# Modulation products in full precision in four column groups of TensorE, with unsplit weights, in the setup and the first retrieval

## The chip, the cores and the metric

The kernel runs on one core of one Trainium2 chip. The metric is the device time of the whole program in microseconds (us). The kernel's time is the median over executions of it.

## The reference, cut to what matters

One inference step of a small trunk with two layers: 128 context tokens and 512 latent tokens, model width 1024. Both layers are modulated: a conditioning vector (`c` for the latent tokens, `c_ctx` for the context tokens) gives shift, scale and gate through a matrix of 1024 x 6144 for each layer.

```python
def _adaln(cvec, w, b):
    mod = jax.nn.silu(cvec) @ w + b
    return jnp.split(mod, 6, axis=-1)

for l in range(DEPTH):
    sh1p, sc1p, g1p, sh2p, sc2p, g2p = _adaln(c_ctx[None, :], ada_w[l], ada_b[l])
    sh1s, sc1s, g1s, sh2s, sc2s, g2s = _adaln(c, ada_w[l], ada_b[l])
    # a token mixer (gated linear recurrence) on the modulated, normed tokens,
    # then the expert mixer on the modulated, normed result:
    #   q = h @ w_q; scores against two sets of 128 sub-keys for each of 8 heads;
    #   top 16 of each, top 16 of the pairs; 16 experts of 16384 per head and token
```

The change touches only how `silu(cvec) @ w` is formed: two vectors against all 6144 columns, once for each layer.

## The kernel before, in words

**Stages.** The program runs stage after stage, with a barrier of all engines between them: `setup`, then for each of the two layers `mixer`, `mix_out`, `retrieve`, `route`, `experts`, and at the end `finish`. In each stage every engine has its own list of instructions and waits on semaphores. SP (the sync engine) only issues transfers, in the order of its list, and a wait in that list holds back every transfer behind it.

**Full float32 products by halves.** A weight tile `w` is split into `hi` (rounded to the format fp32r, on ScalarE) and `lo = w - hi` (on VectorE in `setup`, on GpSimd in `retrieve`), and TensorE multiplies the parts in fp32r. The vectors are split as well: `cs4` holds four columns for each slice of 128 rows, `hi` of both vectors and `lo` of both, so that the modulation's output has four rows (`pa`, `pm`), which a small product with the matrix `fold` adds up and turns into columns (`turn` at L377, `turn_row` at L1655).

**`setup` (L161 to L389).** It loads `ada_w` of layer 0 in 12 blocks of 512 columns (2 MB each) into a ring of four tiles `ada` (L211). From the fifth block on, SP waits until VectorE has made `ada_lo` of the block four before (L209). For each block ScalarE makes `ada_hi` in two halves (`split`, L339), VectorE `ada_lo` in two halves (L316), TensorE 8 + 8 products with a moving operand of 512 columns (L394), ScalarE copies the result row (`mod_row`, L355), TensorE turns it (L382), VectorE adds the bias (L308). Between the blocks ScalarE squares x (L344) and GpSimd adds the squares (L237). Ahead of it, VectorE makes `cs` and `cs4` (L294 to L300), which TensorE waits for.

**`retrieve` of layer 0 (L1451 to L1722).** A head has two steps (b = 0, 1), 16 steps in all; step s = 2h + b. In it TensorE projects all 640 tokens on 128 columns of `w_q`, in two halves of 24 products of 128x320 (P, L497; P of step 0 is at L487), and multiplies the result with the 128 sub-keys (scores S, L1633). VectorE takes the top 16 of the scores (L1683 to L1693), and once per head of the candidate pairs (L1707 to L1716). On the side, the modulation of layer 1 is made in 16 blocks of 384 columns (1.5 MB), one a step: product M (L1651), copy of the row (L1576), turn T (L1659), copy (L1582). In the second retrieval (layer 1, `later` false) this part doesn't exist. The lists are written out by hand:

- TensorE: P(s), S(s-1), M(s-1), P(s+1), S(s), M(s), and so on; T(s-2) stands in the middle of P(s), between its halves (L1623), so right behind M(s-2) come one half of P(s), then T(s-2).
- ScalarE, step s of its loop (L1594): row of M(s-2) (L1576), `ada_hi` of block s (L1570), copy of T(s-2), the copies of the projection of step s, `w_hi` of step s+2 (L1556).
- GpSimd: `ada_lo` (L1536) and `w_lo` (L1530), in turn.
- SP, step s (L1509 to L1520), three transfers: `w_raw` of step s (after `w_lo` of s-2), the keys `kraw`, `ada` of block s (after `ada_lo` of block s-2). Below, D(s) is the transfer of `ada` block s and W(s) that of `w_raw` of step s; W(s+1) stands right behind D(s).

```python
                    if later:
                        sp.wait_ge(ada_lo_done, h * 2 + (b + 1))
                        sp.dma_start(ada[b][:, :, :], ada_w[:, :, bass.ds(h * (2 * AW) + b * AW, AW)]) \
                            .then_inc(ada_in[b], 16)
```

Of the kernel before, what the change touches and what calls it, by code (L numbers as in the profile page):

```python
# [16 lines left out]
P = 128  # L17
# [79 lines left out]
def build_program(nc, a, out, upto=99):  # L97

    x_sp = nc.dram_tensor("xT_spill", [P, DC, T], F32, kind="Internal").ap()
    og_sp = nc.dram_tensor("og_spill", [DC, P, T], F32, kind="Internal").ap()  # L100
    gates_dram = nc.dram_tensor("gates", [KEYS, P, TD], F32, kind="Internal").ap()

    ctx = ExitStack()
    with ctx:
        c = {}
        for name, shape, dt in [
            ("ident", [P, P], F32), ("ones_d", [P, P], F32), ("ones_h", [P, P], F32),
            ("coarse_mask", [P, NT, P], BF16), ("fine_mask", [P, NF, FINE], BF16), ("room", [P, 624], F32),
            ("vec", [P, 3 * P], F32), ("mod", [P, DEPTH, 48, 2], F32), ("one", [P, 1], F32),
            ("scale_w", [P, DC, 2], F32), ("ident_r", [P, P], F32R),  # L110
            ("cs4", [P, DC, 4], F32R), ("fold", [P, 32], F32), ("lb", [P, 16], F32), ("oml", [P, 16], F32),
            ("x", [P, DC, T], F32), ("acc", [P, T], F32), ("inv", [P, PH * NT], F32),
        ]:
# [47 lines left out]
def setup(nc, a, c, x_sp, x_saved):  # L161
# [4 lines left out]
    with ExitStack() as s:  # L166
# [5 lines left out]
        ada_lo = [sb(f"ada_lo{i}", [P, DC, NB], F32R) for i in range(2)]  # L172
        ada_hi = [sb(f"ada_hi{i}", [P, DC, NB], F32R) for i in range(2)]
        cs = sb("cs", [P, 2, DC])
        cs4, fold = c["cs4"], c["fold"][:, 0:2]
# [17 lines left out]
        ada_hi_done, ada_lo_done = sem("ada_hi_done"), sem("ada_lo_done")  # L193
# [9 lines left out]
        HALF_K = (slice(0, DC // 2), slice(DC // 2, DC))  # L203

        @block.sync
        def _(sp):
            for n in range(NALL):
                if n >= 4:
                    sp.wait_ge(ada_lo_done, 2 * (n - 3))  # L209
# [6 lines left out]
        def _(pool):  # L216
# [7 lines left out]
            pool.memset(fold[:, :], 0.0)  # L224
            pool.drain()
            pool.affine_select(out=fold[:, :], in_=fold[:, :], compare_op=ALU.not_equal,
                               fill=1.0, base=0, pattern=[[-1, 2]], channel_multiplier=1)
            pool.drain()
            pool.affine_select(out=fold[:, :], in_=fold[:, :], compare_op=ALU.not_equal,
                               fill=1.0, base=-2, pattern=[[-1, 2]], channel_multiplier=1)  # L230
# [29 lines left out]
        def _(dve):  # L260
# [32 lines left out]
            for v, name in ((0, "c"), (1, "c_ctx")):  # L293
                nc.vector.tensor_mul(cs[:, v, :], sg[:, v, :], c["vec"][:, VEC[name]:VEC[name] + DC])  # L294
            dve.drain()
            for v in range(2):
                nc.vector.tensor_copy(cs4[:, :, v], cs[:, v, :])
            dve.drain()
            for v in range(2):
                nc.vector.tensor_sub(cs4[:, :, 2 + v], cs[:, v, :], cs4[:, :, v].bitcast(F32))  # L300
# [10 lines left out]
            for n in range(NALL):  # L311
                for i, ks in enumerate(HALF_K):
                    dve.wait_ge(ada_hi_done, 2 * n + i + 1)
                    if n >= 2 and i == 0:
                        dve.wait_ge(ada_mm, n - 1)
                    nc.vector.tensor_sub(ada_lo[n % 2][:, ks, :], ada[n % 4][:, ks, :],  # L316
                                         ada_hi[n % 2][:, ks, :].bitcast(F32)).then_inc(ada_lo_done, 1)
                if n >= 2:
                    add_bias(n - 2)
            add_bias(NALL - 2)  # L320
            add_bias(NALL - 1)
# [3 lines left out]
        def _(act):  # L325
# [8 lines left out]
            def split(n):  # L334
                act.wait_ge(ada_in[n % 4], n // 4 * 16 + 16)
                if n >= 2:
                    act.wait_ge(ada_mm, n - 1)
                for ks in HALF_K:
                    act.activation(ada_hi[n % 2][:, ks, :], ada[n % 4][:, ks, :], ACT.Copy).then_inc(ada_hi_done, 1)  # L339

# [5 lines left out]
            split(0)  # L346
            for n in range(NALL):
                if n + 1 < NALL:
                    split(n + 1)
# [5 lines left out]
                act.activation(mod_row[n % 2][0:4, :], pa[n % 2][0:4, :], ACT.Copy).then_inc(row_out, 1)  # L355

        @block.tensor
        def _(pe):
# [18 lines left out]
            def turn(n):  # L377
# [3 lines left out]
                for i in range(NB // P):  # L381
                    last = nc.tensor.matmul(pc[n % 2][:, i, :], mod_row[n % 2][0:4, i * P:(i + 1) * P], fold[0:4, 0:2],  # L382
# [3 lines left out]
            for n in range(NALL):  # L386
                if n >= 2:
                    pe.wait_ge(row_out, n - 1)
                for w, done in ((0, ada_hi_done), (1, ada_lo_done)):  # L389
                    part = (ada_hi, ada_lo)[w][n % 2]  # L390
                    for k in range(DC):
                        if k % 4 == 0:
                            pe.wait_ge(done, 2 * n + k // 4 + 1)
                        last = nc.tensor.matmul(pa[n % 2][0:4, :], cs4[:, k, :], part[:, k, :],  # L394
                                                start=(w == 0 and k == 0), stop=(w == 1 and k == DC - 1))
# [1055 lines left out]
def retrieve(nc, a, c, h_hi, h_lo, chosen, layer):  # L1451
# [10 lines left out]
    with ExitStack() as s:  # L1462
# [27 lines left out]
        if later:  # L1490
            ada_w = a["ada_w"][layer + 1].rearrange("(k p) n -> p k n", p=P)
            ada = [sb(f"ada{i}", [P, DC, AW]) for i in range(2)]
            ada_hi = [sb(f"ada_hi{i}", [P, DC, AW], F32R) for i in range(2)]
            ada_lo = [sb(f"ada_lo{i}", [P, DC, AW], F32R) for i in range(2)]
# [4 lines left out]
            ada_hi_done, ada_lo_done, ada_mm, row_out, row_turned, mod_done = (sem(n) for n in  # L1499
                ("ada_hi_done", "ada_lo_done", "ada_mm", "row_out", "row_turned", "mod_done"))  # L1500
# [7 lines left out]
        def _(sp):  # L1508
            with sp.Fori(0, PH) as h:  # L1509
                for b in range(2):  # L1510
# [6 lines left out]
                    if later:  # L1517
                        sp.wait_ge(ada_lo_done, h * 2 + (b + 1))
# [4 lines left out]
        def _(pool):  # L1523
            pool.sem_inc(w_lo_done, 2)
            if later:
                pool.sem_inc(ada_lo_done, 2)
# [6 lines left out]
            def ada_low(h, b):  # L1533
                if later:
                    pool.wait_ge(ada_hi_done, h * 2 + (b + 1))
                    pool.tensor_tensor(ada_lo[b][:, :, :], ada[b][:, :, :], ada_hi[b][:, :, :].bitcast(F32),  # L1536
                                       ALU.subtract).then_inc(ada_lo_done, 1)

            low(0, 0)
            low(0, 1)  # L1540
            with pool.Fori(0, PH - 1) as h:
                for b in range(2):
                    ada_low(h, b)
                    low(h + 1, b)
            ada_low(PH - 1, 0)
            ada_low(PH - 1, 1)

        @block.scalar
        def _(act):
# [17 lines left out]
            def ada_high(h, b):  # L1567
                if later:
                    act.wait_ge(ada_in[b], h * 16 + 16)
                    act.activation(ada_hi[b][:, :, :], ada[b][:, :, :], ACT.Copy).then_inc(ada_hi_done, 1)  # L1570

            def row(h, b):

                if later:
                    act.wait_ge(ada_mm, h * 2 + (b + 1))
                    act.activation(mod_row[0:4, :], pm[0:4, 0:AW], ACT.Copy).then_inc(row_out, 1)  # L1576
# [13 lines left out]
            for b in range(2):  # L1590
                ada_high(0, b)
                copies(0, b)
                hi(1, b)
            with act.Fori(1, PH - 1) as h:  # L1594
                for b in range(2):
                    row(h - 1, b)
                    ada_high(h, b)
# [3 lines left out]
            for b in range(2):  # L1601
                row(PH - 2, b)
                ada_high(PH - 1, b)
# [7 lines left out]
        def _(pe):  # L1611
            pe.sem_inc(proj, 4)
            pe.sem_inc(k_turned, 2)
            pe.sem_inc(scored, 2)

# [39 lines left out]
            def turn_row(h, b):  # L1655
                if later:
                    pe.wait_ge(row_out, h * 2 + (b + 1))
                    for i in range(AW // P):
                        last = nc.tensor.matmul(turned_row()[:, i, :], mod_row[0:4, i * P:(i + 1) * P], c["fold"][0:4, 0:2],  # L1659
# [755 lines left out]
```

## Time and profile before

| | |
|---|---|
| median of three runs | 4261.61 us (4261.18 to 4262.74) |
| the profiled execution's own time | 4259.91 us |
| its span, first to last instruction | 4258.0 us |
| mean granted TensorE clock | 0.954 of 2.4 GHz |
| busy: TensorE, its weight loads | 3923.1 us (92%), 3549.5 us (83%) |
| busy: VectorE, ScalarE, GpSimd | 3443.8, 1704.9, 1835.2 us |
| `setup` | 0 to 98.4 us |
| `retrieve` of layer 0 | 623.5 to 857.3 us |
| `retrieve` of layer 1 | 2664.8 to 2865.7 us |

"Idle before" a row is what its engine spent waiting ahead of it, with the instruction that ended the wait. PE is TensorE, DVE VectorE, ACT ScalarE, POOL GpSimd; SPq is the sync engine's queue, where a row's duration is only the issue of a transfer.

### The profile page before, as it was taken

To read this page: it belongs to the slowest core of one execution; us is meant where nothing else is said; L and a number is where in the kernel's file an instruction comes from. 1 tells how busy PE (TensorE), PEld (TensorE's weight loads), DVE (VectorE), ACT (ScalarE), POOL (GpSimd) and SP (SyncE) were. 2 spreads that over 40 slices of the span, in tenths; PEclk is the share of its full clock that TensorE was granted. 3 is DMA by queue.
4 is the path that set the end of the run, shared out by engine and by line. 5 is a ranking of instruction groups with operands and counts; after the bars stand their busy time and mean duration, and the time that the engine had idled before them with its cause. 6 is when DMAs were issued, how large, how long until landed. Compare 5 with 4: busy or idle time off the path is not lost. (4 is left out here: it accounts for less than half of the span.)

```text
span 4258.0 us, 75035 instructions
## 1 busy us (share of the span) xinstructions
PE 3923.1 (92%) x25855; PEld 3549.5 (83%) x25855; DVE 3443.8 (81%) x6395; ACT 1704.9 (40%) x2682; POOL 1835.2 (43%) x1261
## 2 busy tenths in 40 slices
PE   6899889878999999999987888858899999999997
PEld 3899888757999999999977888856799999999997
DVE  6565547987888889999986784799788888999997
ACT  6565524354333333333335652216433333333333
POOL 2100037555445455656551003206445454556664
PEclk9999889989999999999998998979999999999999
DMA  7222135349999999999972112205999999999995
GB/s 298 65 70 60 64 107 166 116 103 288 367 362 362 363 362 358 362 362 362 363 272 59 56 48 92 72 17 135 312 362 357 367 361 364 356 362 364 360 362 219
DMA packets 620189, 1049.52 MB, mean 246 GB/s; under 512 B 229763, under 2 KB 405318, under 8 KB 619590
## 3 DMA queue, kind: packets, MB, share of 16 engines
q1 hardware_dynamic: 471520, 508.69, 35.4%
q0 software_dynamic: 147456, 536.94, 34.0%
q10 hardware_dynamic: 1126, 2.79, 0.2%
q8 instruction: 48, 0.79, 0.1%
q14 instruction: 39, 0.32, 0.0%
HBM read 982.75 MB, written 65.54 MB: 246 GB/s over the span
## 5 line engine op out<-in xcount | busy, mean ns | idle before, releaser
L2095 POOL DMA_INDIRECT rows_ex<-in_peer_v,ctx_index x512 | 707.7, 1382 | 476.7 <-DVE row_acc_ex L2174 361.0
L2095 POOL DMA_INDIRECT rows_ex<-in_peer_u,ctx_index x512 | 586.7, 1146 | 636.9 <-DVE dots_ex L2177 502.1
L2260 PE MATMUL pu_ex<-h_hi,uT_hi_ex 128*128 128x384 f32 x2048 | 715.9, 350 | 1.9 <-ACT coef_ex L2124 1.0
L2174 DVE SCALAR_TENSOR_TENSOR row_acc_ex<-rows_ex,factor_ex,row_acc_ex 128x1024 f32<-128x1024 f32 x512 | 658.0, 1285 | 52.8 <-issue 11.1
L2260 PE MATMUL pu_ex<-h_hi,uT_lo_ex 128*128 128x384 f32 x2048 | 693.0, 338 | 0.0
L2260 PE MATMUL pu_ex<-h_lo,uT_hi_ex 128*128 128x384 f32 x2048 | 693.0, 338 | 0.0
L2268 PE MATMUL py_ex<-v_hi_ex,c_hi_ex 128*128 128x512 f32 x1536 | 622.6, 405 | 0.0
L2177 DVE CUSTOM_DVE_ANT_0 rows_ex<-rows_ex,h_row_ex 128x1024 f32<-128x1024 f32 x512 | 604.6, 1218 | 0.0
L2268 PE MATMUL py_ex<-v_lo_ex,c_hi_ex 128*128 128x512 f32 x1536 | 601.3, 391 | 0.0
L2268 PE MATMUL py_ex<-v_hi_ex,c_lo_ex 128*128 128x512 f32 x1536 | 601.1, 391 | 0.0
L2113 ACT ACTIVATE uT_hi_ex<-pT_ex 128x512 fp32r<-128x512 f32 x512 | 303.6, 593 | 509.2 <-PE pT_ex L2253 490.5
L2165 DVE TENSOR_TENSOR uT_lo_ex<-pT_ex,uT_hi_ex 128x512 fp32r<-128x512 f32 x512 | 352.2, 688 | 177.3 <-ACT uT_hi_ex L2113 158.6
L2119 ACT ACTIVATE v_hi_ex<-v_raw_ex 128x1024 fp32r<-128x1024 f32 x256 | 271.7, 1062 | 486.6 <-PE py_ex L2268 486.6
L2260 PEld LDWEIGHTS pu_ex<-h_hi,uT_hi_ex 128*128 128x128 f32 x2048 | 386.0, 188 | 12.8 <-DVE uT_lo_ex L2165 1.5
L2260 PEld LDWEIGHTS pu_ex<-h_lo,uT_hi_ex 128*128 128x128 f32 x2048 | 386.5, 189 | 9.8
L2260 PEld LDWEIGHTS pu_ex<-h_hi,uT_lo_ex 128*128 128x128 f32 x2048 | 385.5, 188 | 0.0
L2268 PEld LDWEIGHTS py_ex<-v_lo_ex,c_hi_ex 128*128 128x128 f32 x1536 | 288.3, 188 | 64.0
L2268 PEld LDWEIGHTS py_ex<-v_hi_ex,c_lo_ex 128*128 128x128 f32 x1536 | 289.5, 188 | 43.2
L2268 PEld LDWEIGHTS py_ex<-v_hi_ex,c_hi_ex 128*128 128x128 f32 x1536 | 288.8, 188 | 42.6
L2188 DVE TENSOR_TENSOR v_lo_ex<-v_raw_ex,v_hi_ex 128x1024 fp32r<-128x1024 f32 x256 | 312.0, 1219 | 0.0
L2253 PE MATMUL pT_ex<-ident,u_raw_ex 128*128 128x128 f32 x2040 | 306.6, 273 | 3.0 <-DVE uT_lo_ex L2165 1.5
L2253 PEld LDWEIGHTS pT_ex<-ident,u_raw_ex 128*128 128x128 f32 x2040 | 254.0, 140 | 47.3 <-DVE uT_lo_ex L2165 3.0
(460 smaller groups left out, 7729.5 us busy)
## 6 DMA issues: line engine op xcount, KB each, us to landing
u_raw_ex<-in_peer_u SPq DMA_DIRECT2D x256, 512.0 KB
v_raw_ex<-in_peer_v SPq DMA_DIRECT2D x256, 512.0 KB
gates<-stage_ro SPq DMA_DIRECT2D x12, 4096.0 KB, 16.0
g_raw_ex<-gates SPq DMA_DIRECT2D x256, 192.0 KB
ada<-in_ada_w SPq DMA_DIRECT2D x12, 2048.0 KB, 12.1
ada_re<-in_ada_w SPq DMA_DIRECT2D x16, 1536.0 KB, 7.0
w_raw_hgrn<-in_hgrn_w_in SPq DMA_DIRECT2D x40, 512.0 KB
w_raw_re<-in_peer_w_q SPq DMA_DIRECT2D x32, 512.0 KB, 4.4
```

Source lines behind the costliest of these rows:

```text
L2095: pool.indirect_dma_start(out=rows[m % RING][:, :], out_offset=None, in_=a["peer_u" if m < TG * NC else "peer_v"].rearrange("l n d -> (l n ...
L2113: act.activation(uT_hi[b][:, 4 * part:4 * part + 4, :], pT[:, :, :], ACT.Copy) \
L2119: act.activation(v_hi[b][:, :], v_raw[b][:, :], ACT.Copy).then_inc(v_hi_done, 1)
L2165: nc.vector.tensor_sub(uT_lo[b][:, at, :], pT[:, :, :], uT_hi[b][:, at, :].bitcast(F32)) \
L2174: nc.vector.scalar_tensor_tensor(row_acc[g][:, :], rows[j][:, :], factor[:, j:j + 1], row_acc[g][:, :], ALU.mult, ALU.add).then_inc(row_fr ...
L2177: nc.vector.tensor_tensor_reduce(rows[j][:, :], rows[j][:, :], h_row[g][:, :], 1.0, 0.0, ALU.mult, ALU.add, accum_out=dots[:, j:j + 1]).th ...
L2188: nc.vector.tensor_sub(v_lo[b][:, :], v_raw[b][:, :], v_hi[b][:, :].bitcast(F32)).then_inc(v_lo_done, 1)
L2253: last_ = nc.tensor.transpose(pT[:, k, :], u_raw[b][:, (4 * part + k) * P:(4 * part + k + 1) * P], c["ident"][:, :])
L2260: last_ = nc.tensor.matmul(pu[:, 0:TD], w[:, k, :], x[:, k, 0:TD], start=(k == 0 and w is uT_hi[b] and x is h_hi), stop=(k == DC - 1 and w ...
L2268: last_ = nc.tensor.matmul(py[2 * t + i][:, :], w[:, t * P:(t + 1) * P], x[:, i * HALF_D:(i + 1) * HALF_D], start=(first and w is c_hi[b] ...
```

## The change

In `setup` and in the first `retrieve` the modulation's weights are no longer split. `cs4` becomes `cs32`: for each slice of 128 rows 32 columns of float32, two of them the vectors and 30 zero. The 8 products of a block are float32 matmuls with 32 output rows each, slice k into the output partitions 32 * (k % 4) and following, so that four of them lie in four column groups of the array; each group adds up two slices (`start=(k < 4)`, `stop=(k >= 4)`). The result has 128 rows, of which two in each group count; `fold` (now over 128 rows) adds the four groups up while it turns. Gone are `ada_hi` and `ada_lo` on ScalarE, VectorE and GpSimd, and their tiles. The waits that hung on them now hang on the product: SP loads the next block into a tile once the product that read it is done (`ada_mm`), in `setup` block n-4, in `retrieve` block s-2; TensorE waits for the transfer itself (`ada_in`).

```diff
         def _(sp):
             for n in range(NALL):
                 if n >= 4:
-                    sp.wait_ge(ada_lo_done, 2 * (n - 3))
+                    sp.wait_ge(ada_mm, n - 3)
...
             for v, name in ((0, "c"), (1, "c_ctx")):
-                nc.vector.tensor_mul(cs[:, v, :], sg[:, v, :], c["vec"][:, VEC[name]:VEC[name] + DC])
-            dve.drain()
-            for v in range(2):
-                nc.vector.tensor_copy(cs4[:, :, v], cs[:, v, :])
-            dve.drain()
-            for v in range(2):
-                nc.vector.tensor_sub(cs4[:, :, 2 + v], cs[:, v, :], cs4[:, :, v].bitcast(F32))
+                nc.vector.tensor_mul(cs32[:, :, v], sg[:, v, :], c["vec"][:, VEC[name]:VEC[name] + DC])
             dve.drain().then_inc(cready, 1)
...
             for n in range(NALL):
                 if n >= 2:
                     pe.wait_ge(row_out, n - 1)
-                for w, done in ((0, ada_hi_done), (1, ada_lo_done)):
-                    part = (ada_hi, ada_lo)[w][n % 2]
-                    for k in range(DC):
-                        if k % 4 == 0:
-                            pe.wait_ge(done, 2 * n + k // 4 + 1)
-                        last = nc.tensor.matmul(pa[n % 2][0:4, :], cs4[:, k, :], part[:, k, :],
-                                                start=(w == 0 and k == 0), stop=(w == 1 and k == DC - 1))
+                pe.wait_ge(ada_in[n % 4], n // 4 * 16 + 16)
+                for k in range(DC):
+                    g = k % 4 * 32
+                    last = nc.tensor.matmul(pa[n % 2][g:g + 32, :], cs32[:, k, :], ada[n % 4][:, k, :],
+                                            start=(k < 4), stop=(k >= 4))
                 last.then_inc(ada_mm, 1)
                 if n >= 1:
                     turn(n - 1)
...
                     if later:
-                        sp.wait_ge(ada_lo_done, h * 2 + (b + 1))
+                        sp.wait_ge(ada_mm, h * 2 + (b + 1))
                         sp.dma_start(ada[b][:, :, :], ada_w[:, :, bass.ds(h * (2 * AW) + b * AW, AW)]) \
                             .then_inc(ada_in[b], 16)
...
             with act.Fori(1, PH - 1) as h:
                 for b in range(2):
                     row(h - 1, b)
-                    ada_high(h, b)
                     turned_copy(h - 1, b)
                     copies(h, b)
                     hi(h + 1, b)
...
             pe.sem_inc(scored, 2)
+            if later:
+                pe.sem_inc(ada_mm, 2)
...
                 if later:
-                    pe.wait_ge(ada_lo_done, h * 2 + (2 + b + 1))
+                    pe.wait_ge(ada_in[b], h * 16 + 16)
                     if not (isinstance(h, int) and h == 0 and b == 0):
                         pe.wait_ge(mod_done, h * 2 + b)
-                    for w, part in enumerate((ada_hi[b], ada_lo[b])):
-                        for k in range(DC):
-                            last = nc.tensor.matmul(pm[0:4, 0:AW], c["cs4"][:, k, :], part[:, k, :],
-                                                    start=(w == 0 and k == 0), stop=(w == 1 and k == DC - 1))
+                    for k in range(DC):
+                        g = k % 4 * 32
+                        last = nc.tensor.matmul(pm[g:g + 32, 0:AW], c["cs32"][:, k, :], ada[b][:, k, :],
+                                                start=(k < 4), stop=(k >= 4))
                     last.then_inc(ada_mm, 1)
```

The order of the lists, where the prediction speaks of it. First ScalarE in the loop of the first retrieval, from the end of one step to the end of the next (`w_hi` is the split of `w_q`, `mod_row` the copied row of the modulation, `mod_raw` its turned copy, `kT` and `qT` the copies for the scores). Before:

```order
L1556 ACTIVATE w_hi_re<-w_raw_re 128x1024
L1575 REGISTER_ALU
L1576 ACTIVATE mod_row_re<-pm_re 4x384
L1570 ACTIVATE ada_hi_re<-ada_re 128x3072
L1582 ISA
L1582 ACTIVATE mod_raw_re<-pm_re 128x6
L1560 REGISTER_ALU
L1561 REGISTER_ALU
L1562 ACTIVATE kT_re<-pk_re 128x128
```

With the change:

```order
L1510 ACTIVATE w_hi_re<-w_raw_re 128x1024
L1524 REGISTER_ALU
L1525 ACTIVATE mod_row_re<-pm_re 128x384
L1529 REGISTER_ALU
L1531 ISA
L1531 ACTIVATE mod_raw_re<-pm_re 128x6
L1514 REGISTER_ALU
L1515 REGISTER_ALU
L1516 ACTIVATE kT_re<-pk_re 128x128
```

`ada_hi` is gone, and `w_hi` of step s+2 still stands ahead of `mod_row` of block s-1. Second, SP's loop of the first retrieval, the same list in both but for line numbers; with the change:

```order
L1477 DMA w_raw_re<-in_peer_w_q 128x8x128
L1480 ISA
L1480 DMA kraw_re<-in_peer_keys 128x128
L1484 ISA
L1484 DMA ada_re<-in_ada_w 128x8x384
L1474 REGISTER_ALU
L1474 COMPARE_AND_BRANCH
```

Nothing moved there; what the transfer of `ada` waits for is another semaphore now, and the next step's `w_raw` is still the transfer behind it.

## Rows read from the trace of the kernel before

**Rows 1.** The page, busy time of each engine, share of the span, instructions.

```profile
PE 3923.1 (92%) x25855; PEld 3549.5 (83%) x25855; DVE 3443.8 (81%) x6395; ACT 1704.9 (40%) x2682; POOL 1835.2 (43%) x1261
```

**Rows 2.** Timeline at setup's first block: start, duration in us, instruction, [idle before].

```profile
31.03 0.24 DVE L294 TENSOR_TENSOR cs<-sg,vec 128x8 f32<-128x8 f32 x2 [0.69 <-ACTq L332]
...
33.14 3.58 PE L394 MATMUL pa<-ada_hi,cs 128*4 128x512 f32 x8 [4.58 <-ACT ada_hi L339]
```

**Rows 3.** SP's timeline and ada landings in setup, windows 37:38 and 71:71.9.

```profile
37.55 0.37 SPq L211 DMA_DIRECT2D ada<-in_ada_w  x1
...
71.53 0.37 SPq L211 DMA_DIRECT2D ada<-in_ada_w  x1
...
DMA to landing us min/median/max: 11.6/11.6/11.6
```

**Rows 4.** Windows of setup: busy us of each engine, granted clock, DMA share, GB/s.

```profile
45.00:65.00 20.00, 20.00 (x102) 9.29 (x100) 19.77 (x15) 18.93 (x16) 2.68 (x1) 1.00 1.05 403
```

**Rows 5.** Timeline at setup's end, ScalarE and VectorE.

```profile
96.11 0.59 ACT L355 ACTIVATE mod_row<-pa 4x512 f32<-4x512 f32 x1 [4.15 <-PE pa L394]
...
97.98 0.17 DVE L308 TENSOR_TENSOR mod<-pc,vec 128x8 f32<-128x8 f32 x1 [0.73 <-PE pc L382]
```

**Rows 6.** Full-precision matmuls: in column groups (L1173, L1183), and over the whole array (L1214).

```profile
175.70 0.27 PE L1158 MATMUL pT_hgrn<-ident,v_hgrn 128*128 128x128 f32 x1
175.90 1.85 PE L1173 MATMUL pS_hgrn<-ex_hgrn 128*64 128x64 f32 x78
...
179.15 1.06 PE L1183 MATMUL pS_hgrn<-ex_hgrn 128*32 128x32 f32 x102 [0.90 <-issue]
...
2337.22 1.03 PE L1214 MATMUL pO_gla<-tt_gla 128*128 128x256 f32 x4
```

**Rows 7.** Timeline of TensorE over one step in the middle of the first retrieval.

```profile
743.90 1.63 PE L1651 MATMUL pm_re<-ada_hi_re,cs 128*4 128x384 f32 x8
745.37 1.55 PE L1651 MATMUL pm_re<-ada_lo_re,cs 128*4 128x384 f32 x8
...
750.47 0.82 PE L1659 MATMUL pm_re<-fold,mod_row_re 4*128 4x2 f32 x6
...
754.85 1.27 PE L1633 MATMUL pS_re<-kT_re,qT_re 128*128 128x128 f32 x10
755.88 1.28 PE L1651 MATMUL pm_re<-ada_hi_re,cs 128*4 128x384 f32 x6
```

**Rows 8.** Second step of the first retrieval: SP's issues, ScalarE, TensorE.

```profile
655.41 0.37 SPq L1519 DMA_DIRECT2D ada_re<-in_ada_w  x1
656.03 0.38 SPq L1512 DMA_DIRECT2D w_raw_re<-in_peer_w_q  x1
...
663.61 1.06 ACT L1556 ACTIVATE w_hi_re<-w_raw_re 128x1024 fp32r<-128x1024 f32 x1 [6.93 <-DMA w_raw_re<-in_peer_w_q]
...
665.09 0.86 PE L1659 MATMUL pm_re<-fold,mod_row_re 4*128 4x2 f32 x6 [1.38 <-ACT mod_row_re L1576]
```

**Rows 9.** Line L1512 in window 740:800, its landings, five issues.

```profile
DMA to landing us min/median/max: 7.4/7.7/7.9
```

**Rows 10.** Windows behind that stop, TensorE: busy (instructions), clock, DMA share, GB/s.

```profile
665.80:669.20 3.40, 3.40 (x13) 0.51 0.82 284
669.20:672.60 3.40, 3.40 (x27) 1.00 1.02 333
```

**Rows 11.** Timeline of TensorE where the second projection starts.

```profile
648.60 0.30 PE L1619 MATMUL pk_re<-ident,kraw_re 128*128 128x128 f32 x1 [0.71 <-ACT kT_re L1562]
```

**Rows 12.** Timeline of VectorE: last head of retrieval 1, one head of retrieval 2.

```profile
836.17 1.09 DVE L1683 MAX8 top_re<-pS_re 128x8 f32<-128x128 f32 x5 [0.36 <-issue]
...
856.66 0.26 DVE L1720 TENSOR_TENSOR mod<-mod_raw_re,vec 128x96 f32<-128x96 f32 x1
...
2767.95 0.30 DVE L1683 MAX8 top_re<-pS_re 128x8 f32<-128x128 f32 x1 [0.30 <-issue]
...
2782.03 0.50 DVE L1683 MAX8 top_re<-pS_re 128x8 f32<-128x128 f32 x2 [0.36 <-issue]
```

More of the change, by code:

```diff
@@ L107, in build_program @@
             ("ident", [P, P], F32), ("ones_d", [P, P], F32), ("ones_h", [P, P], F32),
-            ("coarse_mask", [P, NT, P], BF16), ("fine_mask", [P, NF, FINE], BF16), ("room", [P, 624], F32),
+            ("coarse_mask", [P, NT, P], BF16), ("fine_mask", [P, NF, FINE], BF16), ("room", [P, 422], F32),
             ("vec", [P, 3 * P], F32), ("mod", [P, DEPTH, 48, 2], F32), ("one", [P, 1], F32),
             ("scale_w", [P, DC, 2], F32), ("ident_r", [P, P], F32R),
-            ("cs4", [P, DC, 4], F32R), ("fold", [P, 32], F32), ("lb", [P, 16], F32), ("oml", [P, 16], F32),
+            ("cs32", [P, DC, 32], F32), ("fold", [P, 2], F32), ("lb", [P, 16], F32), ("oml", [P, 16], F32),
             ("x", [P, DC, T], F32), ("acc", [P, T], F32), ("inv", [P, PH * NT], F32),
@@ L171, in setup @@
         ada = [sb(f"ada{i}", [P, DC, NB]) for i in range(4)]
[L172 to L175, printed above, removed]
+        cs32, fold = c["cs32"], c["fold"]
         sg = sb("sg", [P, 2, DC])
@@ L192, in setup @@
             ("ada_mm", "row_out", "row_turned", "mod_done", "iot", "sig", "rows_z", "squared", "gathered"))
-        ada_hi_done, ada_lo_done = sem("ada_hi_done"), sem("ada_lo_done")
         col = 0
@@ L202, in setup @@
         nload = len(loads)
-        HALF_K = (slice(0, DC // 2), slice(DC // 2, DC))
         @block.sync
@@ L224, in _ @@
             pool.memset(fold[:, :], 0.0)
+            pool.memset(cs32[:, :, :], 0.0)
             pool.drain()
[L226 to L230, printed above, removed]
+            for g in range(4):
+                pool.affine_select(out=fold[:, :], in_=fold[:, :], compare_op=ALU.not_equal,
+                                   fill=1.0, base=-32 * g, pattern=[[-1, 2]], channel_multiplier=1)
+                pool.drain()
             pool.affine_select(out=c["ident"][:, :], in_=c["ident"][:, :], compare_op=ALU.not_equal,
@@ L311, in _ @@
             for n in range(NALL):
[L312 to L321, printed above, removed]
+                add_bias(n)
             dve.drain()
@@ L332, in _ @@
             act.drain().then_inc(sig, 1)
[L334 to L339, printed above, removed]
             def square(k):
@@ L344, in square @@
                 act.activation(sq[k % 2][:, :] if k else c["acc"][:, :], xT[:, k, :], ACT.Square).then_inc(squared, 1)
-            split(0)
             for n in range(NALL):
-                if n + 1 < NALL:
-                    split(n + 1)
                 if n >= 4 and n < 4 + DC:
@@ L354, in _ @@
                     act.wait_ge(row_turned, n - 1)
-                act.activation(mod_row[n % 2][0:4, :], pa[n % 2][0:4, :], ACT.Copy).then_inc(row_out, 1)
+                act.activation(mod_row[n % 2][:, :], pa[n % 2][:, :], ACT.Copy).then_inc(row_out, 1)
         @block.tensor
@@ L381, in turn @@
                 for i in range(NB // P):
-                    last = nc.tensor.matmul(pc[n % 2][:, i, :], mod_row[n % 2][0:4, i * P:(i + 1) * P], fold[0:4, 0:2],
+                    last = nc.tensor.matmul(pc[n % 2][:, i, :], mod_row[n % 2][:, i * P:(i + 1) * P], fold[:, :],
                                             start=True, stop=True)
@@ L1492, in retrieve @@
             ada = [sb(f"ada{i}", [P, DC, AW]) for i in range(2)]
-            ada_hi = [sb(f"ada_hi{i}", [P, DC, AW], F32R) for i in range(2)]
-            ada_lo = [sb(f"ada_lo{i}", [P, DC, AW], F32R) for i in range(2)]
             mod_row = sb("mod_row", [P, AW])
@@ L1498, in retrieve @@
             ada_in = [sem(f"ada_in{i}") for i in range(2)]
-            ada_hi_done, ada_lo_done, ada_mm, row_out, row_turned, mod_done = (sem(n) for n in
-                ("ada_hi_done", "ada_lo_done", "ada_mm", "row_out", "row_turned", "mod_done"))
+            ada_mm, row_out, row_turned, mod_done = (sem(n) for n in ("ada_mm", "row_out", "row_turned", "mod_done"))
         def turned_row():
@@ L1524, in _ @@
             pool.sem_inc(w_lo_done, 2)
-            if later:
-                pool.sem_inc(ada_lo_done, 2)
             def low(h, b):
@@ L1531, in low @@
                                    ALU.subtract).then_inc(w_lo_done, 1)
[L1533 to L1537, printed above, removed]
             low(0, 0)
@@ L1542, in _ @@
                 for b in range(2):
-                    ada_low(h, b)
                     low(h + 1, b)
-            ada_low(PH - 1, 0)
-            ada_low(PH - 1, 1)
         @block.scalar
@@ L1565, in copies @@
                     act.activation(qT[b][:, cols], pq[i][:, 0:HALF], ACT.Copy).then_inc(q_out, 1)
[L1567 to L1570, printed above, removed]
             def row(h, b):
                 if later:
-                    act.wait_ge(ada_mm, h * 2 + (b + 1))
-                    act.activation(mod_row[0:4, :], pm[0:4, 0:AW], ACT.Copy).then_inc(row_out, 1)
+                    act.wait_ge(ada_mm, h * 2 + (2 + b + 1))
+                    act.activation(mod_row[:, :], pm[:, 0:AW], ACT.Copy).then_inc(row_out, 1)
             def turned_copy(h, b):
@@ L1590, in _ @@
             for b in range(2):
-                ada_high(0, b)
                 copies(0, b)
@@ L1602, in _ @@
                 row(PH - 2, b)
-                ada_high(PH - 1, b)
                 turned_copy(PH - 2, b)
@@ L1658, in turn_row @@
                     for i in range(AW // P):
-                        last = nc.tensor.matmul(turned_row()[:, i, :], mod_row[0:4, i * P:(i + 1) * P], c["fold"][0:4, 0:2],
+                        last = nc.tensor.matmul(turned_row()[:, i, :], mod_row[:, i * P:(i + 1) * P], c["fold"][:, :],
                                                 start=True, stop=True)
```

## The prediction

> **What bounds the kernel now.** I read the page first: TensorE is busy 92% of the span [rows 1], but nearly all of that lies in stages that the change doesn't touch. Then come the two places where it acts, each by its timeline. The reader should see, in setup, three things that keep almost the same pace: ScalarE and VectorE (18.9 and 19.8 us busy of 20), and the DMA engines (share 1.05, 403 GB/s, so a 2.1 MB block takes 5.2 us) [rows 4]. In the first retrieval TensorE sets the pace in the middle: a step takes 755.88 - 743.90 = 11.98 us [rows 7]. VectorE has 20.9 us of work a head, that is two steps (below), so it is not far behind.
>
> **Setup: -12.5 us.** (a) `cs32` is ready after L294 at 31.3, not after two more rounds and the first `ada_hi`; TensorE starts its first block at 31.4 instead of 33.14 [rows 2]. (b) A block is 8 float32 products, 16 records. Over the whole array a record of 256 columns costs (1.03 - 0.38) / 3 = 0.22 us [rows 6] (0.38 is one record alone), 0.85 ns a column; 512 columns are 0.43 us, 384 are 0.32. In four column groups 102 records of 32 columns came within 1.06 us [rows 6]; less some 0.17 for the last one's tail that is 8.7 ns each against 27 by that price, so at least three of four groups ran at once with records this short, and I take four for long ones: 16 x 0.43 / 4 = 1.7 us a block, twice that at half clock, where the first block lies. It ends at 31.4 + 3.4 + 0.3 = 35.1, and the fifth transfer goes out at 35.3, not 37.55 [rows 3]. (c) From there the transfers run as before: the last was issued at 71.53 and landed 11.6 later, at 83.1, which is 45.5 us after 37.55 [rows 3]; now at 80.8. Block and turn (1.7 + about 1 us, double at half clock) fit into 5.2 us either way. (d) Then one product of 1.9 to 3.7 us (I take 2.7, since half idle engines got either clock), and the tail from row copy to last bias, 98.15 - 96.11 = 2.0 [rows 5]. Setup's work ends at 85.6 instead of 98.15. The splits of the last block on ScalarE and VectorE were in this tail; they hide nothing else. The squares on GpSimd (seven sums) have all the time that the transfers leave. The spill of x, queued behind the last block, lands about when the next stage issues its first weights, which may cost 1 us of this.
>
> **First retrieval: +80 us.** The change takes 2.75 us of `ada_hi` off ScalarE and 6.8 us of `ada_lo` off GpSimd a step. Neither is on the path. It also shortens M from 746.92 - 743.90 = 3.0 us [rows 7] to 16 x 0.32 / 4 + 0.17 = 1.45. All that would be gain. But SP now sends D(s+1) only when M(s-1) is done, and W(s+2) is behind it in SP's list. ScalarE's list has `w_hi` of s+2, which needs W(s+2), ahead of the row of M(s-1); and T(s-1), which needs that row, stands in the middle of P(s+1), the very next thing that TensorE does. So TensorE stops there until two transfers that were only issued at M's end have landed. Before, D(s+1) hung on `ada_lo`, which was made a step ahead of its product.
> The price is in the trace, for this stop occurs once: D at 655.41, W at 656.03, `w_hi` waits 6.93 us for it until 663.61, T starts at 665.09, 9.7 us after D's issue, and TensorE sat idle 1.4 us [rows 8]. In the middle of the stage W lands 7.4 to 7.9 us after its issue [rows 9], so this is no outlier. The step, from the end of one M to the end of the next:
> - 0.2: from M's end to D's issue, an estimate without a row of its own (0 to 0.5 would move the sum by 3 or 4 us);
> - 9.7: D's issue to T [rows 8]. Of it TensorE works 3.7 (one half of P) and idles 6;
> - 4.4: T and the other half, 754.85 - 750.47 [rows 7];
> - 1.0: S, 755.88 - 754.85 [rows 7];
> - 1.45: M, as above;
> - 0.2: into column groups and back: the first grouped matmul started 0.20 us after a whole-array one [rows 6], against about 0.1 between like ones;
> - 2.0: clock. After the stop in rows 8 TensorE was granted 0.51 for 3.4 us and began 13 matmuls, then 27 in the next 3.4 at full clock [rows 10]: 14 x 0.15 (7.2 us for the 48 products of P, below) = 2 us lost. That stop was 1.4 us; these are 6, so I charge it every time.
> Sum 18.95, say 18.9 us, instead of 11.98. The stop comes at each T whose M is followed by a `w_hi`: M(0) to M(12), 13 times.
> End points: P(1) no longer waits 0.7 us for `kT` behind `ada_hi` [rows 11] and starts at 647.8; P without T is 754.85 - 746.92 - 0.7 = 7.2 us [rows 7]; with S, M and a switch, M(0) ends at 657.7. M(13) ends at 657.7 + 13 x 18.9 = 903.4, S(13) 1.4 before, at 902.0. From there VectorE is the path: from a head's second scores to the next head's first 2782.03 - 2767.95 = 14.1, then the last head 856.92 - 836.17 = 20.75 [rows 12]. The stage's work ends at 936.9, instead of 856.92 [rows 12]: +80.
>
> A rule of the Trainium skill weighs against the change: the page "TensorE: Matmul & The Clock Gate", section "Part 3: Packing small matmuls", gives 2.38x for three column tiles at 512 columns, 0.79 of full. Rows 6 leave this open, as their records are short. By that rule M would be 0.35 us longer, and the sum 5 us. The page "TensorEngine Tiling (Array Packing)", "Key Properties", says that a change of tiling mode drains TensorE; the trace agrees, with the 0.20 us above.
>
> **Sum.** 4259.9 (profiled execution) - 12.5 + 80 = 4327.4; the median of the runs is 1.7 above that execution, so 4329 us.
>
> **Bounds of the unknown terms.** Clock: 0 if the stop doesn't lower it (13 x 2.0 = -26), up to half speed through T, half and S (5.4 instead of 2.0, +44; rows 10 show recovery after 3.4 us, so this is far off). Tile switches: 0 to 0.5 us a step, -3 to +4. M: 1.45 if groups overlap fully; 5.3 if not at all. That last is a rival.
>
> **Rivals.**
> 1. *Groups overlap by two only* (two 32-row float32 streams at a time with long operands). For: rows 6 have short records only. Against: 8.7 ns instead of 13.3. M costs 1.3 us more, 13 times 17; in setup first and last block cost 5 more together: 4351 us. Without any overlap, M costs 3.85 more (+50), and a setup block takes 6.8 + 1 us, more than a transfer, ending near 130: 4424 us.
> 2. *Faster: the order doesn't bite.* One mechanism: W(s+2) is in place before ScalarE gets to it, so T never waits, and TensorE's step is 11.98 - 1.55 = 10.4 us. Then VectorE is the bound with 20.9 us a head [rows 12] (14.08 + 6.8), as in the second retrieval: from its second scores at 667 (M(0)'s end, a P with T, S), 7 x 20.9 + 13.9 gives 827, -30, so 4261.6 - 12.5 - 30 = 4219 us. It decides at 2.2 us: W would have to land that soon after M's end, since T comes 3.7 after it and split and row take 1.5. The shortest landing in rows 9 is 7.4. Only a misread list would do it.
> 3. *W overtakes D.* If W needn't wait for D's 1.57 MB, 3.9 us at 403 GB/s [rows 4], it would land 7.7 - 3.9 = 3.8 us after its issue (an estimate); T would wait 2 us, the clock might hold: step 12.9, stage +2, total near 4251 us. Against: [rows 8, 9] have W 7.4 to 7.9 us after issue, with D just ahead.
> 4. *The change doesn't do what it says* (savings in setup swallowed by half clock or the queued spill): setup -6 instead of -12.5. Inside the range.
>
> **How the numbers follow.** The forecast, with its own terms open (4300 without clock loss, to 4345), gets 0.76. Rival 1 gets 0.12, most of it at 4351. Rivals 2 and 3 get 0.07 and 0.03. 0.02 is left for anything near no change. Low is 4298 (no clock loss, cheap switches), high 4356 (two groups only); outside lie the faster cases, no overlap at all, and a worse clock, some 0.17. A difference of 0.2% (8.5 us) is what a measurement of this kernel can tell from none. Faster by that: 0.10; same: 0.02; slower: 0.88.
>
> **What would show each step.** Setup: no `ada_hi`, fifth transfer near 35.3, last bias near 86; matmuls of L362 in fours, 1.7 us a block at full clock. Retrieval: D's issue 0.2 us after M's last record; `w_hi` waiting some 8 us for its transfer in 13 steps; T idle some 6 us behind `mod_row`; granted clock low after each; a step of 18.9 us; VectorE waiting for scores in each; GpSimd nearly idle. The second retrieval and the experts' stages unchanged. It is wrong if the steps of the first retrieval are shorter than 12 us, which would mean that the transfers don't stand in the path, or if M takes over 2.5 us.

## The result and the profile after

| | before | after |
|---|---|---|
| median of the runs | 4262.03 us (4 runs, 4261.18 to 4262.74) | 4347.48 us (4 runs, 4345.74 to 4348.58) |
| profiled execution, span | 4259.9 us, 4258.0 | 4347.0 us, 4345.2 |

The change makes the kernel slower: ratio 1.0199, 95% interval 1.0186 to 1.0212, or +85.4 us, where 4329 (+67) was forecast. Where the time goes is read best from the barriers between the stages (end of each with its barrier, in us from the start):

| end of | before | after | the stage itself |
|---|---|---|---|
| setup | 98.97 | 85.28 | -13.7 |
| first mixer | 523.29 | 510.69 | +1.1 |
| its output product | 623.48 | 610.91 | 0.0 |
| first retrieval | 857.76 | 942.75 | 331.8 instead of 234.3: +97.6 |
| first route | 1018.47 | 1102.21 | -1.2 |
| all the rest | 4257.99 | 4345.19 | +3.5 |

The busy times hide all of this (the page, as [rows 1]): TensorE and VectorE have less to do than before, in a longer span.

```profile
PE 3920.9 (90%) x25855; PEld 3564.7 (82%) x25855; DVE 3356.0 (77%) x6367; ACT 1621.2 (37%) x2642; POOL 1716.0 (39%) x1248
```

**Setup.** The timelines of the changed kernel, VectorE, TensorE and SP at the first block, then TensorE and VectorE at the last (start, duration in us, instruction, [idle before]), as [rows 2, 3, 5]; of the first row's 20 records 16 are the first block:

```profile
31.49 0.25 DVE L289 TENSOR_TENSOR cs<-sg,vec 128x8 f32<-128x8 f32 x2 [0.68 <-ACTq L312]
...
31.82 3.85 PE L362 MATMUL pa<-ada,cs 128*32 128x512 f32 x20 [2.81 <-DVEq L290]
...
35.31 0.37 SPq L206 DMA_DIRECT2D ada<-in_ada_w  x1
...
65.14 3.22 PE L362 MATMUL pa<-ada,cs 128*32 128x512 f32 x16 [2.25 <-DMA ada<-in_ada_w]
...
80.47 1.92 PE L362 MATMUL pa<-ada,cs 128*32 128x512 f32 x16 [0.57 <-DMA ada<-in_ada_w]
...
84.31 0.17 DVE L297 TENSOR_TENSOR mod<-pc,vec 128x8 f32<-128x8 f32 x1 [0.73 <-PE pc L352]
```

The fifth transfer goes out at 35.31, not 37.55. A block takes 1.92 us at full clock; of the eight that wait for their transfer, every other one, from 44.69 on, meets the half clock and takes 3.2 to 3.3 us, and the last one has the full clock. Nothing but the transfer is left ahead of the last one, which starts at 80.47; the last bias is there at 84.5 instead of 98.15.

**First retrieval.** One step of the changed kernel, in the timelines of TensorE, SP and ScalarE. M ends, D is issued 0.19 us later and W 0.91 behind it; W lands 7.8 us after its issue (7.4 to 8.0 from M(0) on, median 7.7), and ScalarE has waited for it for 11 us with M's finished row behind `w_hi` in its list. T comes 10.5 us after M's end:

```profile
743.09 1.50 PE L1599 MATMUL pm_re<-ada_re,cs 128*32 128x384 f32 x16
...
744.78 0.37 SPq L1484 DMA_DIRECT2D ada_re<-in_ada_w  x1
745.69 0.37 SPq L1477 DMA_DIRECT2D w_raw_re<-in_peer_w_q  x1
...
753.56 1.06 ACT L1510 ACTIVATE w_hi_re<-w_raw_re 128x1024 fp32r<-128x1024 f32 x1 [11.04 <-DMA w_raw_re<-in_peer_w_q]
754.52 0.47 ACT L1525 ACTIVATE mod_row_re<-pm_re 128x384 f32<-128x384 f32 x1
...
755.05 1.44 PE L1607 MATMUL pm_re<-fold,mod_row_re 128*128 128x2 f32 x6 [6.68 <-ACT mod_row_re L1525]
```

The windows of one step (length; busy us and instructions of PE, PEld, DVE, ACT, POOL; granted clock; DMA share; GB/s) show what follows the stop: TensorE works 6.9 us at the lower of its clocks before the clock is back (4.5 to 7.3 us in the 13 steps, 6.7 in the mean).

```profile
744.70:755.00 10.30, 3.67 (x25) 3.41 (x24) 9.81 (x69) 1.43 (x2) 0.31 (x1) 0.84 0.64 210
755.00:761.94 6.94, 6.89 (x27) 6.89 (x28) 1.80 (x14) 0.77 (x3) 2.05 (x1) 0.50 0.00 0
761.94:764.70 2.76, 2.76 (x31) 2.03 (x29) 0.81 (x4) 0.44 (x1) 0.00 (x0) 1.00 0.00 0
```

The waits from M(0)'s end to M(13)'s (us in total, times, longest) say it for all 13 steps, and show VectorE waiting in each for its scores:

```profile
ACT w_hi_re L1510 <- DMA w_raw_re<-in_peer_w_q: 140.4, 13, 11.3
DVE top_re L1631 <- PE pS_re L1581: 135.4, 13, 14.0
...
PE pm_re L1607 <- ACT mod_row_re L1525: 83.7, 13, 6.9
```

### The profile page after: what moved, and what is told of

It is laid out like the page before. It is cut to its first block and busy times, and to the rows that moved or that the text cites. A ratio compares the mean times of both kernels' runs of the same rounds, so it can differ in the third digit from the quotient of the medians.

```text
span 4345.2 us, 74929 instructions
## 1 busy us (share of the span) xinstructions
PE 3920.9 (90%) x25855; PEld 3564.7 (82%) x25855; DVE 3356.0 (77%) x6367; ACT 1621.2 (37%) x2642; POOL 1716.0 (39%) x1248
```

## The experiments

All are edits of the changed kernel, except the last, and ran beside the kernel before, whose medians there were 4260.1, 4262.5 and 4265.9 us.

### Which order makes the stop

**D behind W.** The list of SyncE (SP) only:

```diff
-            with sp.Fori(0, PH) as h:
-                for b in range(2):
-                    (W(h, b), K(h, b), D(h, b))
+            weights(0, 0)
+            with sp.Fori(0, PH - 1) as h:
+                weights(h, 1)
+                block_of_ada(h, 0)
+                weights(h + 1, 0)
+                block_of_ada(h, 1)
+            weights(PH - 1, 1)
+            block_of_ada(PH - 1, 0)
+            block_of_ada(PH - 1, 1)
```

(`weights` holds the wait and issue of W and of K, `block_of_ada` those of D, unchanged.)

> In SyncE's list D(s) goes out behind W(s+1) and K(s+1), not ahead of them; it still waits for M(s-2). My theory (the stop is W held back behind D's wait, with w_hi ahead of the row in ScalarE's list): W is in place a step earlier, T waits for nothing, TensorE's step is about 10.6 us, VectorE becomes the bound at 20.9 us a head, the first retrieval lasts about 204 us instead of 331.8, and the time is 4347.5 - 128 = 4220 us (4212 to 4232). Rival (the two ada buffers themselves are the limit: a transfer that may start only when M(s-2) is done comes too late for M(s)): the step stays near 20 us and the time near 4347. Second rival (the float32 products in column groups are what is slow, by tile switches or by what they do to the clock): TensorE's step stays over 14 us, and the time over 4260.

4218.32 us, ratio 0.9904 (0.9890 to 0.9917): faster than both kernels. The first retrieval takes 205.1 us, every step from M's end to M's end 10.5. ScalarE's wait for W is down to 0.21 us, in its timeline:

```profile
705.55 1.06 ACT L1521 ACTIVATE w_hi_re<-w_raw_re 128x1024 fp32r<-128x1024 f32 x1 [0.21 <-DMA w_raw_re<-in_peer_w_q]
707.48 0.49 ACT L1536 ACTIVATE mod_row_re<-pm_re 128x384 f32<-128x384 f32 x1 [0.87 <-PE pm_re L1610]
```

Behind a D, W still takes 7.3 to 8.7 us to land (median 7.6); it only starts a step earlier. The windows from M(0)'s end to M(13)'s, of this kernel and of the change:

```profile
644.33:781.01 136.68, 136.68 (x1054) 121.98 (x1055) 121.77 (x803) 34.69 (x77) 30.07 (x13) 1.00 0.63 202
```

```profile
644.98:908.38 263.40, 179.72 (x1055) 161.60 (x1055) 121.75 (x803) 34.34 (x78) 30.54 (x13) 0.75 0.34 107
```

The same 13 steps take 127 us less, which is all of the difference between the two retrievals (331.8 - 205.1). In the change TensorE stands still for 84 of its 263 us and works 43 us longer on the same products, at a mean clock of 0.75; here it is never idle, and VectorE, which was expected to be the bound, waits 6.3 us for it in 7 waits. Both rivals fall: neither two buffers nor the float32 products need more than this.

**W first, but as late.** The same list, with the wait of D ahead of W:

```diff
             def weights(h, b):
-                sp.wait_ge(w_lo_done, h * 2 + (b + 1))
+                sp.wait_ge(ada_mm, h * 2 + b)
```

(the first three W keep the old wait).

> As the run before, but W(s+1) also waits for M(s-2), as it did behind D: it goes out 0.2 us after M and no longer has D's 1.57 MB ahead of it. If D's bytes are what W waits for, W lands 3.8 us after its issue instead of 7.7, T waits 1.8 us, the step is 12.9 to 14 us, the first retrieval about 240 to 255 us, and the time 4256 to 4270. If the landing time of W is its own and not D's, T comes 9.4 us after M instead of 10.5, the step is 19 us, and the time 4347.5 - 13 x 1.1 = 4333.

4271.19 us, ratio 1.0019 (1.0009 to 1.0028), first retrieval 255.5 us, 14.4 us a step. W is issued 0.2 us after M and lands 3.7 us later (3.7 to 4.5 in the stage); the stop is 1.7 us in the step shown, where 1.8 were worked out, and 1.6 to 2.6 in the 13 steps. Step, stage and time lie just above the ranges that were given:

```profile
740.02 0.83 PE L1625 MATMUL pm_re<-fold,mod_row_re 128*128 128x2 f32 x6 [1.73 <-ACT mod_row_re L1543]
```

So half of W's 7.7 us are D's bytes ahead of it. The clock falls in 12 of the 13 steps even here; the window behind T, as above:

```profile
741.20:744.70 3.50, 3.50 (x16) 3.50 (x15) 0.62 (x5) 0.57 (x2) 0.83 (x1) 0.51 0.51 188
```

**Row ahead of w_hi.** ScalarE's list only (one of the two rounds of the loop; the ends follow it):

```diff
-                    row(h - 1, b)
-                    turned_copy(h - 1, b)
-                    copies(h, b)
-                    hi(h + 1, b)
+                row(h - 1, 0)
+                hi(h, 1)
+                turned_copy(h - 1, 0)
+                copies(h, 0)
```

> SyncE's list as in the change; in ScalarE's list the row of M(s-2) now stands ahead of w_hi of s+1 instead of behind it. My theory: T finds its row at once (it comes 1.5 us after M), but P(s+1) now waits for its own w_lo: M(s-2), D 0.2, W 0.9, landing 7.7, w_hi 1.1, w_lo 3.3 makes 13.2 us, then P, S, M of 10 us, for two steps: 11.6 us a step, 12 to 13.6 with clock lost in that new wait. The first retrieval lasts 225 to 255 us and the time is 4240 to 4270. Rival (SyncE's order alone makes the stop, ScalarE's place plays no part): the step stays near 20 us and the time near 4347.

4232.70 us, ratio 0.9934 (0.9919 to 0.9950), first retrieval 217.6 us, 11.5 us a step. `w_hi` still waits 8 us for W, but no row stands behind it, and the next projection misses its `w_lo` by 0.6 us only. That is faster than the range that was expected (4240 to 4270, 225 to 255 us): `w_lo` was put at 3.3 us and takes GpSimd 2.4, and a wait of 0.6 us never lowered the clock. To mend either order alone removes nearly all of the stop. So the stop needs both: W behind D, and the row behind `w_hi`.

### What a step's 20.3 us are made of

**T behind the second half of P.**

```diff
-                    if i == 1 and turns:
-                        turn_row(h - 1, b)
                     pe.wait_ge(q_out, h * 4 + (1 + 2 * b + i))
                     split_product(...).then_inc(proj, 1)
+                    if i == 1 and turns:
+                        turn_row(h - 1, b)
```

> The change with T moved from between the two halves of P to behind the second one. SyncE's and ScalarE's lists are as in the change. If the step is the chain M, D's issue, W's landing, w_hi, row, T, then S and M, with the second half of P now beside it: 10.4 + 0.8 + 1.0 + 1.5 + 0.4 = 14.1 us, 15.8 if T, S and M run at half clock; the first retrieval lasts 254 to 276 us and the time is 4270 to 4291. Rival (a stop costs what it costs wherever it stands, since the transfers are late by a fixed time behind P): no change from 4347.

4290.16 us, ratio 1.0069 (1.0052 to 1.0085), first retrieval 273.1 us, 15.7 us a step. The chain through both lists is the same length, with 3.6 us more of TensorE's work beside it; the stop is down to 2.6 us (2.4 to 2.8, but for the first, of 3.9):

```profile
766.38 1.05 PE L1606 MATMUL pm_re<-fold,mod_row_re 128*128 128x2 f32 x6 [2.59 <-ACT mod_row_re L1525]
```

**The stop filled.**

```diff
                     if i == 1 and turns:
+                        if later:
+                            pe.wait_ge(q_out, h * 4 + (1 + 2 * b + i))
+                            for _ in range(26):
+                                nc.tensor.matmul(pq[i][:, 0:P], c["ident"][:, :], c["ident"][:, :],
+                                                 start=True, stop=True)
                         turn_row(h - 1, b)
```

> The change, with 26 float32 products of the identity (128 columns, about 0.21 us each, 5.5 us together at full clock) ahead of T in the first retrieval, into the PSUM tile that P's second half overwrites: they fill the stop and add nothing to the result. Theory (the term for the clock was too small: half clock holds over T, P's second half and on, some 3 us a step): TensorE stays at full clock, T comes 10.4 us after M as before, the step falls from 20.1 to 17.3 us, the first retrieval lasts 295 us, and the time is 4311 us. Rival (the step's extra 1.2 us is in the transfers or in the products, not in the clock): the step stays at 19.5 us or more, the time at 4338 or more.

4313.98 us, ratio 1.0120 (1.0103 to 1.0136), first retrieval 297.3 us. Useless work made the change 34 us faster. A window of two steps has a granted clock of 1.00:

```profile
704.00:738.00 34.00, 32.99 (x267) 30.36 (x266) 19.09 (x126) 5.31 (x12) 4.74 (x2) 1.00 0.39 127
```

After two first steps of 19.7 us, in which the clock still fell once each, a step is 17.0 us. So the clock costs about 3 us of a step (20.3 - 17.0 = 3.3, and 43 / 13 = 3.3 by the windows further up), where the forecast had 2.0.

### What the column groups bring

On the kernel with D behind W, in setup and first retrieval (the copy of the result row and the turn shrink from 128 rows to 32 with it):

```diff
                     for k in range(DC):
-                        g = k % 4 * 32
-                        last = nc.tensor.matmul(pm[g:g + 32, 0:AW], c["cs32"][:, k, :], ada[b][:, k, :],
-                                                start=(k < 4), stop=(k >= 4))
+                        last = nc.tensor.matmul(pm[0:32, 0:AW], c["cs32"][:, k, :], ada[b][:, k, :],
+                                                start=(k == 0), stop=(k == DC - 1))
```

> The kernel in which D goes out behind W, with the eight products of a block one after the other in rows 0 to 31 of the array instead of in four column groups (setup and first retrieval). By the price for the whole array, 0.43 us a record of 512 columns and 0.32 of 384, M takes 5.3 us instead of 1.5, TensorE's step 14.3 instead of 10.5, the first retrieval 255 us instead of 205; a block in setup takes 6.9 us and its turn 1, more than the transfer's 5.2, and setup ends near 130 instead of 85.2. Time 4218 + 50 + 45 = 4313 us. Rival (without groups the chip overlaps the streams by itself, the groups bring little): within 15 us of 4218.

4320.18 us, ratio 1.0137 (1.0120 to 1.0153), 99 us more by the ratios than with groups: setup ends at 128.7 instead of 85.3, the first retrieval takes 260.5 instead of 205.1, M 5.35 us instead of 1.50. The group of M's records in the middle of the retrieval:

```profile
L1608 PE MATMUL pm_re<-ada_re,cs 128*32 128x384 f32 x193 | 64.7, 488 | 0.0
```

64.7 / 193 = 0.335 us a record; with groups 1.50 / 16 = 0.094, the last one's tail included. Four streams of 384 columns run side by side.

### Setup alone, and an effect of where a tile lies

The new setup with the old first retrieval needs both sets of constants:

```diff
+            ("cs32", [P, DC, 32], F32), ("fold", [P, 2], F32), ("cs4", [P, DC, 4], F32R), ("fold4", [P, 2], F32),
-            ("room", [P, 624], F32),
+            ("room", [P, 390], F32),
```

> The new setup with the first retrieval as it was (cs4 and the old fold are made beside cs32 on VectorE and GpSimd, off the path). If the two halves of the change are independent, setup ends 13.7 us earlier, the mixer gives 1.1 back, the retrieval lasts its old 234.3 us, and the time is 4262.0 - 12.6 = 4249.4 us. If the retrieval's loss came in part from what setup leaves behind (layout, shifted stages), the retrieval would be longer than 234.3 here too, and the time over 4252.

4285.04 us, ratio 1.0055 (1.0038 to 1.0073): slower than either reading had it. Setup ended at 87.5 us and the retrieval took 236.6, each some 2 us over what was expected; the loss lay in the two route stages, 173.7 and 175.2 us instead of 160.5. The transfers there, in the DMA view of the first route stage:

```profile
gates<-stage_ro SPq DMA_DIRECT2D x6, 4096.0 KB, 20.8
```

Before and in the change it is 16.0. I took it for the place of the tiles and moved them, by too little:

> The run with the new setup and the old first retrieval again, with the tile of spare room 8 bytes smaller, so that all later tiles lie 32-byte aligned as in the kernel before. There the two route stages had 173.7 and 175.2 us instead of 160.5, and their stores to gates took 20.8 us instead of 16.0. If that was the alignment of the stores' source, both route stages return to 160.5, and the time is 13.2 + 14.7 = 28 us less than that run's 4285.0: 4257, or up to 5 us less if the other stages' shifts go too. If something else in it slows the routes, it stays at 4285.

4281.19 us, ratio 1.0048 (1.0032 to 1.0065): the routes still 173.5 and 173.9. The 8 bytes had vanished in the filling up to 32; the source tiles began at byte 101920 in both.

> The new setup with the old first retrieval a third time. In both runs before it the two tiles that the route stages store to gates began 32 bytes above their place in the kernel before and in the change (byte 101920 of a partition instead of 101888); taking 8 bytes off the spare room had not moved them, since each tile is filled up to 32 bytes. Here the spare room is 32 bytes smaller again and they begin at 101888. If the 20.8 us of a store instead of 16.0 come from the place of its source, the stores take 16.0 us again, the route stages 160, and the time is 4281.2 - 13.0 - 13.4 = 4255 us or, if the longer setup (89.3 us instead of 85.2) was that too, 4250. If the place plays no part: 4281, routes of 173.

(`room` of 380 columns.) 4248.55 us, ratio 0.9963 (0.9949 to 0.9977). The stores take 16.0 us again and the routes 159.8:

```profile
gates<-stage_ro SPq DMA_DIRECT2D x6, 4096.0 KB, 16.0
```

So the setup half of the change alone is worth 15.8 us by the ratio (10 to 22 by the interval), which the 12.6 us of the stages fit; the profiled executions differ by 12.2. The place of the tiles had cost 36 by the ratios, 28 of it in the two routes. This run differs from the one before by 32 bytes of spare room alone, so the place is the cause. That it is the place of these two tiles, and not of another tile behind the spare room, is read from the stores' own times.

**The order without the change.** The kernel before with D behind W:

> The kernel before (split weights, single-pass products), with only the order of SyncE's list changed: D(s) behind W(s+1) and K(s+1). It separates what the order gives by itself from what the unsplit products give once the order is mended. My theory: before the change TensorE's 11.98 us a step were the pace and W came in time but once, so the order gives only that one stop (about 3 us with its clock): 4259 to 4263 us, and the 29 us of the mended change in the first retrieval belong to the products. Rival (the order alone makes the retrieval shorter): first retrieval near 205 to 215 us instead of 234.3, 4235 to 4243 us.

4258.58 us, ratio 0.9986 (0.9977 to 0.9996); first retrieval 229.8 us, all of its steps 11.98 and the first one no longer 14.9. The order gives the one stop of [rows 8] back, 2.95 us. The other 1.5 of the 4.5 us lie ahead of M(0)'s end, where the mean granted clock was 0.81 here and 0.72 before; whether the order did that is open. The other 24.7 us of the mended change's retrieval, 229.8 - 205.1, come with the unsplit products.

## Why the prediction came out as it did

The sign, the mechanism and the range held; the forecast was 18 us short, nearly all of it in one stage. By the profiled executions it is 19.6 us: 17.6 in the first retrieval, and 2 in the stages behind it, which the change doesn't touch.

- **Setup, -12.5.** Measured: stage -13.7, first mixer +1.1, together -12.6. That this meets the -12.5 so closely is luck: two misses of 1.1 us cancel. Setup's last product took 1.92 us, not the 2.7 that were put between its two possible values; every other block ran at half clock, and the last one happened to have the full one. That, and a transfer that landed 0.3 us sooner, is the extra 1.1 of the stage. The mixer's 1.1 was named as what a queued spill might cost, but was not in the sum; no run here separates it, and that stage takes 424.8 to 426.6 us in the ten other runs, 426.6 with the old setup. Fifth transfer 35.3, measured 35.31.
- **M, 1.45.** 1.50. All four groups overlap, as taken; rival 1 is refuted, and its price without any overlap, M at 5.3 us and setup near 130, is what the ungrouped run shows (5.35, 128.7). The Trainium skill's page "TensorE: Matmul & The Clock Gate", "Part 3: Packing small matmuls", has 2.38x for three column tiles; four here give 5.35 / 1.50 = 3.6x with the tail in it, 0.89 of full and not 0.79, so the trace bears out about half of that loss at most.
- **The stop.** It comes 13 times, at M(0) to M(12), as read from the two lists. M(0) ends 34.1 us into the stage (34.2 by the forecast), the tail from M(13) to the last bias is 33.5 us (33.5).
- **The step, 18.9.** Measured 263.4 / 13 = 20.26. Means of the 13: M to D 0.20 (0.2); D to T 10.02 (9.7; SyncE issues W 0.62 and 0.91 us behind D in turn, and the row taken had 0.62); T and the other half of P 7.34 (4.4 + 2.0); S, M and switches 2.71 (2.65). **The step that failed is the clock's 2.0 us.** It was taken from [rows 10], behind a stop of 1.4 us, with the words "these are 6, so I charge it every time": the number of stops was scaled, the length was not. Behind stops of 6.2 to 6.9 us TensorE worked 6.7 us at half clock in the mean, not 3.4. The term was 2.9 us, 13 x 0.94 = 12 of the 17.6 us; the longer way from D to T is 4 more. The filled stop confirms it: 3 us a step come back with the clock.
- **Rival 2, 4219 us.** Not what the change does, but what it does once W isn't behind D: 4218, with TensorE at 10.5 us a product and never idle, and VectorE, which this rival had as the bound, just within that. **Rival 3**'s price for W, 3.8 us, holds once W is ahead of D: 3.8 is the median there. Its step of 12.9 us was too short (14.4), mainly by the clock, which stops of 1.6 to 2.6 us lowered in 12 of 13 steps; it had put "the clock might hold".

## What to carry to other kernels

A wait that is moved to a later event holds back all that stands behind it in its queue. Here TensorE's 84 us of standing still came not from the buffer whose wait was moved, but from the next transfer behind it, and only because another engine's list had work of the finished product behind work that needs that transfer; look for that pair, and put the transfer that the nearest step needs ahead of the one that waits. Price a stop of TensorE by its length twice: once for standing still, once for the clock, whose cost grows with the stop. Full-precision products with few rows are worth their column groups: 0.094 us a record instead of 0.335.

## What was not expected of the hardware

- **The place of a store's source.** Six stores of 4 MB a stage, in pieces of 256 bytes, took 16.0 us each at up to 290 GB/s from tiles that begin at byte 101888 of a partition (a multiple of 256), and 20.8 us at 218 GB/s from byte 101920, 32 bytes on. Nothing in the two stages' code differed, and each lost 13 to 15 us. Which multiple it takes wasn't tried.
- **Half clock against length of stop.** In the first retrieval, 13 stops of 1.6 to 2.6 us (W first) left the granted clock at half for 3.4 us nine times, for 6.8 three times, and once not at all. With 13 stops of 2.4 to 3.9 us (T behind P) it was three, eight and two. With the change's stops of 6.2 to 6.9 us it was 10.2 each time but the first (6.8), 3.4 of it in the stop of the step shown. So the length of a stop shifts the odds and doesn't fix the cost. With 10.5 us steps and no stop it never fell, nor did it with the twelve waits of 0.6 us and the one of 1.9 of the row ahead of `w_hi`.
- **W behind D.** 0.5 MB landed 3.7 to 4.5 us after its issue without D ahead of it (W first) and 7.4 to 8.0 behind D's 1.57 MB on the same queue (the change, from M(0) on).
